# All rows of the second expert table summed on TensorE in PSUM

## What is computed

```python
def peer_ffn(h, p):
    def one_block(xb):
        q = (xb @ p['peer_w_q']).reshape(TOKEN_BLOCK, PEER_HEADS, 2, PEER_HALF)
        ...
        gate = jax.nn.softmax(fv, -1)
        act = jax.nn.gelu(jnp.einsum('thkd,td->thk', p['peer_u'][eid], xb))
        return jnp.einsum('thk,thkd->td', gate * act, p['peer_v'][eid])
    ...
x = layer_norm(ALPHA * x + g2 * peer_ffn(x * (1 + sc2) + sh2, p), p['ln2_g'], p['ln2_b'])
```

## Time and profile before

| | |
|---|---|
| median of three executions | 5474.67 us |
| profiled execution | 5474.31 us, its span from first to last instruction 5472.5 us |
| mean granted TensorE clock | 0.759 of 2.4 GHz |
| TensorE busy | 3114.8 us (57% of the span) |
| VectorE busy | 3448.9 us (63%) |
| ScalarE busy | 629.9 us (12%) |
| GpSimd busy | 2849.7 us (52%) |
| DMA | 1667.46 MB, mean 305 GB/s |

### The profile page before, as it was taken

One profiled execution on the slowest core, in us unless ns is written; L12 is line 12 of the kernel. 1 busy time (PEld: TensorE's weight loads), 2 busy tenths in 40 slices (PEclk: granted clock), 3 DMA queues, 4 the chain that ended last, 5 costly groups with the idle time before them and its releaser, 6 DMA issues. The chain is left out here.

```text
span 5472.5 us, 35115 instructions
## 1 busy us (share of the span) xinstructions
PE 3114.8 (57%) x9560; PEld 1611.1 (29%) x9560; DVE 3448.9 (63%) x6879; ACT 629.9 (12%) x1577; POOL 2849.7 (52%) x2830
## 2 busy tenths in 40 slices
PE   5647756357455645647545576655564564565354
PEld 1333334134123323411223233332232341233111
DVE  1255556666776856764468555567686677768765
ACT  0100121111011111000011001101101101111000
POOL 0015635366555645645446364445564665556675
PEclk9768858678677867878768787677786786777777
DMA  7537778789888988989888778768898898889998
GB/s 256 217 139 263 249 290 297 271 313 349 325 311 338 334 303 292 369 296 352 317 326 306 266 245 318 260 244 318 333 347 311 302 367 314 310 343 332 361 380 325
DMA packets 438293, 1667.46 MB, mean 305 GB/s; under 512 B 53072, under 2 KB 66448, under 8 KB 427504
## 3 DMA queue, kind: packets, MB, share of 16 engines
q0 software_dynamic: 369920, 1346.02, 67.1%
q1 hardware_dynamic: 68192, 319.31, 15.2%
HBM read 1637.48 MB, written 36.57 MB: 306 GB/s over the span
## 5 line engine op out<-in xcount | busy, mean ns | idle before, releaser
L559 PE MATMUL ps<-ring,diag 128*128 128x512 f32 x2560 | 1554.4, 757 | 1184.2 <-ACT diag L533 762.1
L490 POOL DMA_INDIRECT ring<-in_peer_v,eid_s x1280 | 1359.8, 1062 | 1080.0 <-PE ps L559 456.2
L490 POOL DMA_INDIRECT ring<-in_peer_u,eid_s x1280 | 1333.1, 1041 | 838.2 <-DVE dots L591 487.2
L591 DVE CUSTOM_DVE_ANT_0 ring<-ring,ps 128x1024 f32<-128x1024 f32 x1104 | 1305.7, 1217 | 124.2 <-DMA ring<-in_peer_u,eid_s 113.0
L559 PEld LDWEIGHTS ps<-ring,diag 128*128 128x128 f32 x2560 | 580.7, 241 | 2014.4 <-issue 1281.1
L601 DVE SCALAR_TENSOR_TENSOR acc<-ring,wsel,acc 128x1024 f32<-128x1024 f32 x640 | 827.4, 1293 | 484.5 <-DMA ring<-in_peer_v,eid_s 436.7
L855 PE MATMUL ps<-W,hT 128*128 128x512 f32 (+1 forms) x800 | 334.6, 581 | 60.6 <-DMA W<-in_w_in 44.2
L533 ACT ACTIVATE diag<-ident,wsel 128x128 f32<-128x128 f32 x640 | 225.4, 395 | 710.6 <-DVE wsel L584 393.8
L1192 PEld LDWEIGHTS ps<-hT,W 128*128 128x128 f32 x2560 | 294.5, 193 | 32.6 <-issue 17.7
L1192 PE MATMUL ps<-hT,W 128*128 128x128 f32 x2560 | 296.5, 277 | 11.6 <-ACT hT L1248 11.6
L591 DVE CUSTOM_DVE_ANT_0 ring<-ring,x2e 128x1024 f32<-128x1024 f32 x176 | 218.9, 1282 | 99.1 <-DMA ring<-in_peer_u,eid_s 98.8
(11 more groups left out here) (203 smaller groups left out, 2849.1 us busy)
## 6 DMA issues: line engine op xcount, KB each, us to landing
W<-in_w_q SPq DMA_DIRECT2D x28, 2048.0 KB, 14.8
W<-in_w_ada SPq DMA_DIRECT2D x24, 2048.0 KB
W<-in_w_out SPq DMA_DIRECT2D x10, 4096.0 KB, 27.0
W<-in_w_in SPq DMA_DIRECT2D x16, 2048.0 KB, 16.2
ring<-in_peer_u,eid_s POOLq DMA_INDIRECT x1280, 6.4
ring<-in_peer_v,eid_s POOLq DMA_INDIRECT x1280, 6.1
xs<-x_state SPq DMA_DIRECT2D x20, 512.0 KB, 3.6
toep<-mod_rows SPq DMA_DIRECT2D x20, 512.0 KB, 7.9
```

The costliest lines, as they stand in the source:

```text
L490: pool.indirect_dma_start(ring[:, r % RING, :], None, a["peer_u"] if kind == "u" else a["peer_v"], bass.IndirectOffsetOnAxis(ap=eid_s[:, h ...
L559: last = pe.matmul(acc_ps[:, c * 512:(c + 1) * 512], diag[:, (E.by_pe[r] - 1) % DIAGS, :], ring[:, r % RING, c * 512:(c + 1) * 512], start ...
L591: dve.tensor_tensor_reduce(out=ring[:, r % RING, :], in0=ring[:, r % RING, :], in1=x2, scale=1.0, scalar=0.0, op0=ALU.mult, op1=ALU.add, a ...
```

## The change

`on_pe` now sends every v row to TensorE. VectorE keeps the dot products and the weights. The sum in SBUF is gone: nothing zeroes `acc`, TensorE does not copy it to PSUM, and the first v row of a block starts the sum in PSUM itself (`start=first`). So that it does not overwrite a sum that is still to be read, it waits for the first link of the previous block's closing, which now multiplies straight out of PSUM. `acc` stays as the buffer of the closing.

```diff
--- before.py
+++ after.py
@@ -57,7 +57,6 @@
 
 RING = 8
 HEAD_ROWS = 2 * TOPK
-BY_PE = 2
 DIAGS = 4
 SHORT_TURN = 4
 
@@ -84,7 +83,7 @@
 
 
 def on_pe(kind, k):
-    return kind == "v" and k % BY_PE == 0
+    return kind == "v"
 
 
 class Experts:
@@ -344,7 +343,6 @@
         e_in = sem("e_in")
         x2_copied = sem("x2_copied")
         ids_staged = sem("ids_staged")
-        acc_zero = sem("acc_zero")
         used_dve = sem("used_dve")
         used_pe = sem("used_pe")
         gelu_sel = sem("gelu_sel")
@@ -422,12 +420,16 @@
         def last_sum(dve, tiles):
 
             link = chain(dve, end_chain)
-            link(dve.tensor_tensor(acc[:, :], acc[:, :], acc_ps, ALU.add))
             dve.wait_ge(end_in, 64)
-            link(dve.tensor_tensor(acc[:, :], acc[:, :], tiles[1], ALU.mult))
+            link(dve.tensor_tensor(acc[:, :], acc_ps, tiles[1], ALU.mult))
             link(dve.scalar_tensor_tensor(acc[:, :], tiles[0], ALPHA, acc[:, :], ALU.mult, ALU.add))
             layer_norm(link, dve, acc[:, :], tiles[2], tiles[3], tiles[0], st12e, mve, vee[:, :], rstde[:, :],
                        end_var, end_rstd, 1).then_inc(end_done, 1)
+
+        def first_v_waits(pe, E):
+
+            if E.ended is not None:
+                pe.wait_ge(end_chain, 1)
 
         def last_sum_rstd(pool):
             pool.wait_ge(end_var, 1)
@@ -447,10 +449,6 @@
             if E is not None and E.begin:
                 if E.ended is not None:
                     last_sum(dve, ended_tiles)
-
-                    dve.wait_ge(end_done, 1)
-
-                dve.memset(acc[:, :], 0.0).then_inc(acc_zero, 1)
 
         def experts_sync_end(sp, E):
             if E is None:
@@ -545,19 +543,14 @@
                     r = at[0]
                     kind, h, k = E.order[r]
                     if on_pe(kind, k):
-                        if at[1]:
-
-                            at[1] = False
-                            pe.wait_ge(acc_zero, 1)
-                            for c in range(2):
-                                zeroed = pe.matmul(acc_ps[:, c * 512:(c + 1) * 512], ident[:, :], acc[:, c * 512:(c + 1) * 512],
-                                                   start=True, stop=False, skip_group_check=True)
-                            zeroed.then_inc(acc_zero, 1)
+                        first, at[1] = at[1], False
+                        if first:
+                            first_v_waits(pe, E)
                         pe.wait_ge(gath[r % RING], E.landed(r))
                         pe.wait_ge(diag_done, E.by_pe[r])
                         for c in range(2):
                             last = pe.matmul(acc_ps[:, c * 512:(c + 1) * 512], diag[:, (E.by_pe[r] - 1) % DIAGS, :],
-                                             ring[:, r % RING, c * 512:(c + 1) * 512], start=False, stop=False, skip_group_check=True)
+                                             ring[:, r % RING, c * 512:(c + 1) * 512], start=first, stop=False, skip_group_check=True)
                         last.then_inc(used_pe, 1)
                     at[0] += 1
             return rows
@@ -565,7 +558,7 @@
         def experts_vector(dve, E, in_psum=False):
             if E is None:
                 return lambda share: None, lambda: None
-            at = [0, E.begin]
+            at = [0]
             x2 = x2_ps if in_psum else x2e[:, :]
 
             def rows(share):
@@ -579,27 +572,16 @@
                     if kind == "v" and k == 0:
 
                         if h >= 2:
-                            dve.wait_ge(diag_done, (h - 1) * TOPK // BY_PE)
+                            dve.wait_ge(diag_done, (h - 1) * TOPK)
                         dve.wait_ge(gelu_sel, h + 1)
                         dve.tensor_tensor(wsel[:, h % 2, :], gel[:, h % 2, :], gates_e[:, ds((E.first + h) * TOPK, TOPK)], ALU.mult).then_inc(w_ready, 1)
                         dve.wait_ge(w_ready, h + 1)
                     if not on_pe(kind, k):
                         dve.wait_ge(gath[r % RING], E.landed(r))
-                        if kind == "u":
-                            if k == 0 and h >= 2:
-                                dve.wait_ge(gelu_sel, h - 1)
-                            dve.tensor_tensor_reduce(out=ring[:, r % RING, :], in0=ring[:, r % RING, :], in1=x2, scale=1.0, scalar=0.0,
-                                                     op0=ALU.mult, op1=ALU.add, accum_out=dots[:, h % 2, k:k + 1]).then_inc(used_dve, 1)
-                        else:
-                            if at[1]:
-
-                                dve.wait_ge(acc_zero, 2)
-                                at[1] = False
-
-                            if E.by_dve[r] > 1:
-                                dve.wait_ge(used_dve, E.by_dve[r] - 1)
-                            dve.scalar_tensor_tensor(acc[:, :], ring[:, r % RING, :], wsel[:, h % 2, k:k + 1], acc[:, :],
-                                                     ALU.mult, ALU.add).then_inc(used_dve, 1)
+                        if k == 0 and h >= 2:
+                            dve.wait_ge(gelu_sel, h - 1)
+                        dve.tensor_tensor_reduce(out=ring[:, r % RING, :], in0=ring[:, r % RING, :], in1=x2, scale=1.0, scalar=0.0,
+                                                 op0=ALU.mult, op1=ALU.add, accum_out=dots[:, h % 2, k:k + 1]).then_inc(used_dve, 1)
                     at[0] += 1
 
             def finish():
```

## The result

Four executions of the changed kernel took 5840.53 to 5863.96 us, median 5854.71, against 5474.53 of four executions before: ratio 1.0698, 95% interval 1.0676 to 1.072. The forecast was 5658, slower, with a range up to 5770. The direction was right; the loss, 380 us, is twice the forecast's 184. The profiled execution of after is the one of 5863.96 us, 390 above the one of before, with a mean granted clock of 0.824. One execution of the last kernel of this document, of nine, took 6917 us and is not in its ratio.

What follows compares the result with a forecast made beforehand. Gathers bound the experts-only step; TensorE's in-order program bounds input-step ends and the modulation step; both balance in the query projection. 124 + 27.5 + 18 + 15 + 1 - 1.2 = 184 us on 5474.3 gives 5658 us, range 5560 to 5770.

Steps and rivals of the forecast that it cites:

- Input steps: Nine input steps: eight rows more in TensorE's chain at 1.72 us, 13.8 us each, 124 us slower together.
- Modulation step: Second modulation step: 16 rows in an unbroken TensorE chain, 27.5 us slower, from 20 to 40.
- the sort's "-17": Sort of eight-head steps: VectorE's program 30.8 us shorter, but 107 us of transfers remain, so 17 us gained a step.
- Their start, -4 us: Start of eight-head steps: closing loses a VectorE add and four TensorE records setting the PSUM sum, 4 us gained.
- heads, output projection and norm, +10: Eight-head steps before the query projection: +5 us for output projection and layer norm, +5 for the heads.
- Query projection: Query projection of eight-head steps: eight rows more on TensorE, 13.8 us slower a step, while gathers can't use the time.
- Steps of four and five heads: Three steps with four, four and five heads: 23 us lost ahead of the sort, 18 gained in it, +5 each.
- Experts-only step: Experts-only step: DMA-bound; last 16 rows cost +5 us, less 4 for the closing, so +1.
- VectorE did hold the gathers a little: First rival: VectorE holds the gathers back; freed, eight-head steps gain up to 52 us each; 5350 us, chance 0.07.
- the low clock: Second rival: a row costs up to 3.44 us in the heads and experts-only step; 5910 us, chance 0.09.
- The balance: Third rival: the sorts' gains come in full and pay for the input steps; 5474 us, chance 0.04.
- The signs: Profile marks for right (input step about 85 us, projection DMA share under 0.85) or wrong (eight-head steps over 20 us off).

Runs made afterwards that it cites:

- the last kernel of this document: Kernel before, v rows on VectorE in second modulation step and eight-head query projection, on TensorE in turns of two in experts-only step: 5452.11 us, ratio 0.9968.
- the first of the three kernels: Against the kernel before, all v rows on TensorE only in rows 0 to 147 of the six eight-head steps: 5534.34 us, ratio 1.0126.

## Why the prediction was wrong

- Input steps: right in mechanism and size, 13.8 us each, +124.6 against +124.
- Modulation step: 27.5 forecast, 17.6 measured. In the step of the earlier trace rows, TensorE's timeline before has two waits for scaled matrices that those rows leave out, the first ahead of a slow burst (two rows in 5.31 us, where 3.44 are the rule):

```profile
2536.55 5.31 PE L559 MATMUL ps<-ring,diag 128*128 128x512 f32 x8 [11.20 <-ACT diag L533]
...
2576.37 2.74 PE L559 MATMUL ps<-ring,diag 128*128 128x512 f32 x4 [2.56 <-ACT diag L533]
```

  The chain was not unbroken, so a part of the added rows may have filled such time; no run tests that.
- Eight-head steps, the step that failed: the sort's "-17". I read that VectorE's program would be 31 us shorter and set it against the transfers (107 of 124 us), but put TensorE's 24 more rows there at nothing: a row on TensorE holds its buffer 1.72 us, the gathers then wait for TensorE, and behind VectorE's routing TensorE still has rows to do. In the changed kernel the sort with its tail measured +3.6 (8.9 us earlier on VectorE, 12.6 later on TensorE), so 20.6 us a step, 124 of the 206 us between the forecast and the profiled execution. The rows that would have said so were in the trace of before: in that window GpSimd waited 13.6 us for TensorE, against 5.6 + 2.7 for VectorE.
- Their start, -4 us, and heads, output projection and norm, +10: together +3.5 up to the query projection against 6 forecast; the start alone brought nothing. Query projection +13.8: right for its own rows (+13.4), but +21.0 in full, 43 us more over six steps; the 7.4 us that the rows of the heads cost there were not in the sum. That the first of the three kernels lost 11.2 in all, near the forecast's 10, is luck.
- Steps of four and five heads: the four-head steps lost 24.5 us ahead of the sort (forecast 23) and won 13 in it (18). The step of five heads lost 38 ahead of its sort, 27 of it in the query projection, and won 1 in it; I had put all three at one value, and no run takes this step apart.
- Experts-only step: +1 forecast, +23 measured. I took 1.43 us a gather for the rate of the transfers, because the DMA share was 0.98. With rows of half the length the same step took 346.5 us, and on GpSimd's timeline in its middle the gathers go out 1.24 to 1.25 us apart:

```profile
5040.56 0.94 POOL L488 DMA_INDIRECT ring<-in_peer_u,eid_s  x1 [0.30 <-issue]
5041.80 0.94 POOL L488 DMA_INDIRECT ring<-in_peer_u,eid_s  x1 [0.30 <-issue]
5043.05 0.94 POOL L488 DMA_INDIRECT ring<-in_peer_u,eid_s  x1 [0.30 <-issue]
```

  So 366 was not the gathers' time. What it was, GpSimd shows in the 200 us from 5150 before: its issues with the idle time before them fill the window, and almost none of that is a wait for a buffer.

```profile
L490 POOL DMA_INDIRECT ring<-in_peer_u,eid_s x75 | 81.9, 1092 | 22.9 <-issue 19.8 <-DVE dots L591 1.8 <-POOL eid_s L481 1.4
L490 POOL DMA_INDIRECT ring<-in_peer_v,eid_s x72 | 72.3, 1004 | 23.4 <-issue 20.8 <-PE ps L559 2.6
```

  GpSimd's own issuing set the pace there, so each wait for TensorE's longer runs of rows counted. In the changed kernel, from 5516 to 5716, these waits are

```profile
POOL ring L488 <- PE ps L552: 37.4, 42, 2.2
```

  against 2.6 us before; turns of two took 27 us of the step back.
- The rivals: VectorE did hold the gathers a little, but freeing it by means of TensorE gave that away; the clock rose (0.75 to 0.84 in the eight-head step, 0.73 to 0.83 in the experts-only step), so the low clock added nothing to the loss: of the v rows' matmul records 496 of 1536 lasted over 1 us in the eight-head steps before, 363 of 3072 after. The balance did not come about.
- The range's ends for the eight-head steps (-20 to +25 a step) left out +28, and the sort, given as a gain alone, had no losing end of its own in the working. The upper end of the three smaller steps is +60 by the bounds given (25 less 5, three times), not +30; with it the range would end at 5765 us, which changes nothing.
- The signs: the input step's came (84.7 us), the modulation step's, the query projection's DMA share and the sort's did not (216 us for 226; 0.93; 127.6 us for 124.0 in the step of the earlier trace rows, at a DMA share of 0.80). Of those for being wrong, two came: 28 us more for an eight-head step, and 389 us for the experts-only step. The third, a clock below 0.8 in the heads, came as a mean over all heads of that step (0.76, before 0.68), but not in its later part (0.88 from 1629 to 1790).

## What to carry to other kernels

Where several engines feed from one ring of buffers, price a moved operation by how long it holds its buffer on the new engine against the pace of the transfers, not only by what the old engine saves. Ask of the stretch that should gain who frees the buffers there. And a busy share of 1 on a queue is not its best rate, nor a sign that the transfers set the pace: look at what the engine that issues them waits for, and for the bytes per second of a stretch in which nothing disturbs it.

## What was unexpected of the hardware

At a DMA share of about 1, two rates stand: 384 GB/s in the experts-only step before, 408 GB/s with rows of half the length on TensorE and none on VectorE. Windows of 200 us each, before and then the latter:

```profile
DMA packets 21060, 76.71 MB, mean 384 GB/s; under 512 B 2342, under 2 KB 2342, under 8 KB 21054
```

```profile
DMA packets 22380, 81.53 MB, mean 408 GB/s; under 512 B 2488, under 2 KB 2488, under 8 KB 22373
```

With VectorE's rows, an issue on GpSimd takes up to 1988 ns, and at most 972 without (ns min/median/max in the same windows):

```profile
L490 POOL DMA_INDIRECT ring<-in_peer_u,eid_s x75: 933/937/1988, 5149.9 to 5349.2; - x75
```

```profile
L488 POOL DMA_INDIRECT ring<-in_peer_u,eid_s x77: 937/941/972, 4941.2 to 5136.7; - x77
```

What goes with the longer issue is a second SBUF input on VectorE, as the earlier trace rows showed for one row. In the whole trace of before, 257 of 621 issues beside a row of line 601, whose tensors all lie in SBUF, took over 1.1 us; of those beside a dot product, 40 of 76 where the token is read from SBUF, and none of 848 where it is read from PSUM. The Trainium skill (SBUF — State Buffer, "Who interferes with whom") infers that an instruction which takes only the shared read interface does not hold up the writing of descriptors. The trace speaks against it.

From 384 to 408 GB/s is 6%, about 12 of 200 us. In the first window the 67 issues beside a row of line 601 took 16.2 us in sum above 0.94 us each, which is enough for that step, as an estimate. TensorE's shorter rows can't be its reason, as GpSimd waited 2.6 us for TensorE's rows in the first window and 12.4 in the second. The changed kernel with whole rows in turns of two, without rows on VectorE, reached 400 GB/s in such a window.
